# Routing and first-expert gather of a hybrid trunk step: sample tiles taken ahead of the prompt tile, rows gathered from the residual stream

## The chip, the cores and the metric

The kernel runs on one core of one Trainium2 chip. The metric is the device time of one execution in microseconds (us). TensorE, VectorE, ScalarE, GpSimd and SyncE are called PE, DVE, ACT, POOL and SP, as in the profile.

## The reference

One layer of a trunk over 640 tokens of width 1024: 128 prompt tokens and 512 sample tokens, five tiles of 128. The part that matters here begins at the output projection of the token mixers:

```python
x = x + g1 * mix
h2 = _rms_norm(x, p['norm2_g']) * (1 + sc2) + sh2
x = x + g2 * _expert_choice_ffn(h2, p)

logits = (h @ p['w_router']).astype(jnp.float32) + p['b_router'].astype(jnp.float32)
aff = jax.nn.softmax(logits, axis=-1)
gate, idx = lax.top_k(aff.transpose(0, 2, 1), cap)
xs = jax.vmap(lambda hb, ib: hb[ib])(h, idx)
gg = jnp.einsum('becd,edf->becf', xs, p['w_e_gate'])
uu = jnp.einsum('becd,edf->becf', xs, p['w_e_up'])
y = jnp.einsum('becf,efd->becd', jax.nn.silu(gg) * uu, p['w_e_down']) * gate[..., None].astype(h.dtype)
```

Scale and shift (sc2, sh2, g1, g2) differ between prompt and sample. Each of 16 experts takes the 64 sample tokens and the 16 prompt tokens with the highest affinity for it, 80 rows in all, and its weights are 12 MB of float32.

## The kernel before, in words

The order of the work is written out by hand, one instruction stream for each engine, with semaphores between them. A float32 product is made of three products of a high and a low part (`mm3`, lines 1812 to 1814): a high part is a copy on ACT, a low part a subtraction on DVE or POOL.

**Projection.** `w_out` comes in four units of 256 columns. `token_major("out", u, t)` makes one unit for one tile in 24 products; DVE's `residual` (1510 to 1520) multiplies by the gate into `otmp` and adds that to the residual stream `X2`. The last ten jobs follow `OUT_LAST` (97). Between them PE turns each tile's `X2` in two halves (`turn_x2`, 2191), ACT (`first_half`) and DVE (`turned`, 1522) copy these to `x2T`, and `route` (2207) multiplies them by the scaled router matrix into bank 7. The order of tiles is `TILE_ORDER`, the prompt tile last.

**Normalisation.** ACT's `sum_squares` gives each tile's sum, POOL's `rstd2` (648) the reciprocal root. `h2t` is made by DVE for the first three tiles (`modulated`, 1529), and for the other two by POOL and ACT: `scaled` (655), `normalise` (1070), `shifted` (661). ACT stores `X2` (`store_x`, 1077) and `h2t` (`store_h`, 1081) to memory; the later experts gather from there.

**Routing.** One `softmax` (1536) on DVE serves the five tiles and ACT's `softmax_exp` stands in its middle. PE turns the affinities of the first expert into rows (2285), DVE counts for each token how many are ahead of it (`ranks`, 1631) and makes one-hot matrices `hot` and `hot_w`. PE multiplies them with `h2t`: the prompt rows in one step (2295), the sample rows in partial sums (2305) that ACT copies to `parts` (1118) and PE turns and adds (2312). ACT copies the result to `x0f` (`x_raw`, 1120) and its high part to `xTh` (`x_hi`, 1125); DVE makes the low part `xTl` from the bank and `xTh` (`x_lo`, 1625). For the other experts DVE searches the highest values eight at a time (`search`, 1661; 1663 to 1666), and `x_lo(0)` stands after the fifth search.

**First expert.** Units 0, 1 and 5 of the twelve weight units are multiplied in full float32 (`raw_unit`, 2322, line 2329). Units 2, 3 and 4 follow in split form (`gate_up`, 2353). Each waits on `e_lo` for its low part, and these three low parts are POOL's:

```python
            gp.wait_ge(s_idx, 3)
            first_lo(2)
            gp.wait_ge(s_gx, 2)
            for b in range(4):
                gp.wait_ge(s_hst[b], 32 if b == 0 else 16)
            first_lo(3)
            first_lo(4)
```

The buffers of units 3 and 4 lie where `h2t` was, so `first_lo(3)` waits until all five stores of `h2t` have landed (`s_hst`, the fifth tile counted on `s_hst[0]`). SP loads the weight units in order (528 to 551): unit 4 after the last projection, unit 9 after the stores and `s_gx`. `turn_lists` stands in unit 4, after its second chunk.

Of the kernel before, what the change touches and what calls it, by code (L numbers as in the profile page):

```python
# [21 lines left out]
P = 128  # L22
# [21 lines left out]
WARM_0, WARM_A, WARM_B = 14, 1, 6  # L44
# [52 lines left out]
OUT_LAST = [(2, 0), (2, 1), (3, 0), (2, 2), (3, 1), (2, 3), (3, 2), (2, 4), (3, 3), (3, 4)]  # L97
# [73 lines left out]
def trunk(nc, a, outs, consts, scratch):  # L171
# [25 lines left out]
    with ExitStack() as ctx:  # L197
# [126 lines left out]
        TOLD = (7808, 7168, 8752, 9392, 10032)  # L324
# [168 lines left out]
        def _(sp):  # L493
# [34 lines left out]
            def expert(e):  # L528
                first = isinstance(e, int) and e == 0
                for k in (2, 3, 0, 1, *range(4, 12)) if first else range(12):  # L530
# [6 lines left out]
                    elif not first:  # L537
                        sp.wait_ge(e_lo, 12 * e + (k - 11 - len(RAW)))
                    elif k < 2:
                        lo_ready(sp, U_OF[("out", 2 + k)])  # L540
                    elif k == 2:
                        unit_used(sp, U_OF[("conv", 1)])
                    elif k == 4:
                        unit_used(sp, N_U - 1)
                    elif k == 9:
                        sp.wait_ge(s_hst[3], 16)
                        sp.wait_ge(s_xst, 16 * TT)
                        sp.wait_ge(s_t2, 2 * TT)
                        sp.wait_ge(s_nm, 2)
                        sp.wait_ge(s_gx, 2)  # L550
# [19 lines left out]
        def _(gp):  # L570
# [174 lines left out]
        def _(act):  # L745
# [314 lines left out]
            def softmax_exp():  # L1060

                act.wait_ge(s_mx2, 1)
                act.activation(aff[:, 0:TT, 0:E_N], lgs, ACT.Exp).then_inc(s_ex2, 1)
# [17 lines left out]
            def store_h(i):  # L1081
# [3 lines left out]
                else:  # L1085
                    act.wait_ge(s_h2p, 5 - i)
                act.dma_start(h2_d[t * P:(t + 1) * P, :], h2t[i]).then_inc(s_hst[i % 4], 16)

            def first_half(i):
# [3 lines left out]
                act.copy(x2T[:, i % 2], bank[4 + i % 2][:, :].rearrange("p (c t) -> p c t", c=4)).then_inc(s_t2a, 1)  # L1093

# [6 lines left out]
            for i in range(1, 4):  # L1101
                act.wait_ge(s_ssq, TT + i)
                sum_squares(i)
                store_x(i)
                store_h(i - 1)
            act.wait_ge(s_ssq, TT + 4)
            sum_squares(4)
            normalise(3)
            softmax_exp()
            normalise(4)  # L1110
            store_x(4)
            e_hi_unit(0, 2)
            store_h(4)
            e_hi_unit(0, 3)
            store_h(3)
            for hf in range(2):
                act.wait_ge(s_gx, hf + 1)
                act.copy(parts[:, 512 * hf:512 * hf + 512], bank[4 + hf][:, :]).then_inc(s_gs, 1)

            def x_raw():  # L1120
                for hf in range(2):
                    act.wait_ge(e_xt, hf + 1)
                    act.copy(x0f[:, 4 * hf:4 * hf + 4, :], bank[6 + hf][:, 0:4 * M_E].rearrange("p (c t) -> p c t", c=4)).then_inc(e_xr, 1)
# [58 lines left out]
            x_raw()  # L1182
            e_hi_unit(0, 4)
            act.wait_ge(s_hst[0], 32)
            x_hi(0)
# [21 lines left out]
        def _(dve):  # L1207
# [302 lines left out]
            def residual(i, t):  # L1510
# [3 lines left out]
                cols = slice(256 * i, 256 * i + 256)  # L1514
                dve.wait_ge(s_job, n + 1)
                dve.scalar_tensor_tensor(otmp[:, n % 2, :], bank_a(n)[:, 0:256], 0.5, g1bc[:, g, cols], ALU.mult,
                                         ALU.mult).then_inc(s_jd, 1)
                dve.wait_ge(s_jd, freed(n)[1])
                ins = dve.tensor_tensor(X2[:, t, cols], X2[:, t, cols], otmp[:, n % 2, :], ALU.add)
# [16 lines left out]
            def softmax():  # L1536

                y = aff[:, 0:TT, 0:E_N]

                def spread(c):  # L1540
                    return stat[:, c:c + TT].unsqueeze(2).to_broadcast([P, TT, E_N])
# [3 lines left out]
                link(dve.tensor_tensor(lgs, bank[7][:, 0:ROUTE_N * TT].rearrange("p (t e) -> p t e", t=TT)[:, :, 0:E_N], spread(10), ALU.mult))  # L1545
                link(dve.tensor_tensor(lgs, lgs, lb5, ALU.add))
                link(dve.tensor_reduce(stat[:, 36:36 + TT], lgs, AX, ALU.max, negate=True))
                dve.tensor_tensor(lgs, lgs, spread(36), ALU.add).then_inc(s_mx2, 1)
                dve.wait_ge(s_ex2, 1)
                link(dve.tensor_reduce(stat[:, 41:41 + TT], y, AX, ALU.add))  # L1550
                link(dve.reciprocal(stat[:, 46:46 + TT], stat[:, 41:41 + TT]))
                dve.tensor_tensor(y, y, spread(46), ALU.mult).then_inc(s_aff, 1)
# [56 lines left out]
            turned(1)  # L1609
            residual(2, TILE_ORDER[4])  # L1610
            modulated(2)
            residual(3, TILE_ORDER[3])
            turned(2)
            residual(3, TILE_ORDER[4])
            turned(3)
            turned(4)
            softmax()


# [11 lines left out]
            def ranks(t, row, n):  # L1631
# [3 lines left out]
                told = fa[:, TOLD[t]:TOLD[t] + width + P]  # L1635
# [3 lines left out]
                ins = dve.scalar_tensor_tensor(told[:, width:], row[:, n:n + P], v, low, ALU.is_equal, ALU.mult,  # L1639
# [9 lines left out]
            ranks(0, bank[1][:, 0:P], 0)  # L1649
            link(dve.tensor_reduce(rank[:, 0:1], above[:, 0, :], AX, ALU.add))  # L1650
            dve.tensor_tensor(hot_w, slot_p, rank[:, 0:1].to_broadcast([P, CAP_S]), ALU.is_equal).then_inc(s_idx, 1)
            for b in range(2):
                for i in (b, b + 2):
                    ranks(1 + i, bank[0], P * i)
                link(dve.tensor_reduce(rank[:, 1 + b:TT:2], above[:, 1 + b:TT:2, :], AX, ALU.add))
                dve.tensor_tensor(hot[:, b:TT - 1:2, :], slot_p.unsqueeze(1).to_broadcast([P, 2, CAP_S]),
                                  rank[:, 1 + b:TT:2].unsqueeze(2).to_broadcast([P, 2, CAP_S]), ALU.is_equal).then_inc(s_idx, 1)
            dve.wait_ge(s_affp, 2)
            link(dve.tensor_copy(affT, bank[2][0:96, 0:256]))
# [8 lines left out]
            for r in range(CAP_S // 8 - 1):  # L1668
                if r == 5:
# [3 lines left out]
                    x_lo(0)  # L1673
                search(r)

# [133 lines left out]
        def _(pe):  # L1809
# [202 lines left out]
            def token_major(kind, i, t, u):  # L2012
# [5 lines left out]
                for dc in range(DC):  # L2018
                    if kind == "out" and i == 0 and t == TILE_ORDER[0]:
                        pe.wait_ge(s_h, DC + dc + 1)  # L2020
                    last = mm3(bank_a(n)[:, 0:256], hTh[:, dc, x], hTl[:, dc, x], wh[:, dc, :], wl[:, dc, :], dc == 0,
                               dc == DC - 1)
                last.then_inc(s_job, 1)
# [167 lines left out]
            def turn_x2(k, i):  # L2191
# [10 lines left out]
                for c in range(4):  # L2202
                    dc = 4 * k + c
                    last = pe.transpose(bank[4 + q % 2][:, c * P:(c + 1) * P], X2[:, t, dc * P:(dc + 1) * P], ident[:, :])
                last.then_inc(s_t2, 1)

            def route(k, i):
# [6 lines left out]
                for c in range(4):  # L2214
                    x = E_N * ((DC if t == 0 else 0) + 4 * k + c)
                    n = ROUTE_N if x + ROUTE_N <= 2 * DC * E_N else E_N
                    last = pe.matmul(bank[7][:, ROUTE_N * t:ROUTE_N * t + n], x2T[:, q % 2, c, :], wr2f[:, x:x + n],
                                     start=k == 0 and c == 0 and i == 0, stop=k == 1 and c == 3 and i == 4)
# [24 lines left out]
            def last_out(n):  # L2243
# [3 lines left out]
                token_major("out", u, TILE_ORDER[i], out_2 + u - 2)  # L2247
# [12 lines left out]
            last_out(5)  # L2260
            route(0, 4)
            turn_x2(1, 0)
            last_out(6)
            route(1, 0)
            turn_x2(1, 1)
            last_out(7)
            route(1, 1)
            last_out(8)
            turn_x2(1, 2)
            last_out(9)  # L2270
            route(1, 2)
            turn_x2(1, 3)
            turn_x2(1, 4)
            route(1, 3)
            route(1, 4)

            def warm(n, b=1):
# [3 lines left out]
            warm(WARM_0)  # L2281
            pe.wait_ge(s_aff, 1)
            for t in (1, 2, 3, 4, 0):
                out = bank[1][:, 0:P] if t == 0 else bank[0][:, P * (t - 1):P * t]
                last = pe.transpose(out, aff[:, t, 0:1].to_broadcast([P, P]), ident[:, :])
            last.then_inc(s_affp, 1)
            for rows, col, t in ((0, 0, 1), (0, 1, 2), (32, 0, 3), (32, 1, 4), (64, 0, 0), (64, 1, TT)):
                last = pe.matmul(bank[2][rows:rows + 32, col * P:(col + 1) * P], aff[:, t, :], ident[:, :], start=True, stop=True)
            last.then_inc(s_affp, 1)
            warm(WARM_B, 5)  # L2290
            pe.wait_ge(s_idx, 1)
            pe.wait_ge(s_h2p, 1)
            for c in range(DC):
                x0 = (c % 4) * M_E + CAP_S
                pe.matmul(bank[6 + c // 4][:, x0:x0 + CAP_S], h2t[4][:, c * P:(c + 1) * P], hot_w, start=True, stop=True)
                if c % 2 == 1:
                    warm(WARM_A)
            for i in range(2):
                pe.wait_ge(s_idx, 2 + i)
                if i == 1:  # L2300
                    pe.wait_ge(s_h2p, 2)
                for hf in range(2):
                    for g in range(4):
                        tile = i if g < 2 else 2 + i
                        last = pe.matmul(bank[4 + hf][32 * g:32 * g + 32, :], hot[:, tile, 32 * (g % 2):32 * (g % 2) + 32],
                                         h2t[tile][:, 512 * hf:512 * hf + 512], start=i == 0, stop=i == 1)
                    if i == 1:
                        last.then_inc(s_gx, 1)
            for hf in range(2):
                pe.wait_ge(s_gs, hf + 1)  # L2310
                for c in range(4):
                    last = pe.matmul(bank[6 + hf][:, c * M_E:c * M_E + CAP_S], parts[:, (4 * hf + c) * P:(4 * hf + c + 1) * P], twice,
                                     start=True, stop=True)
                last.then_inc(e_xt, 1)

            def first_lists():
                pe.matmul(bank[3][CAP_S:M_E, 0:2], hot_p, aff[:, 0, 0:2 * E_N:E_N], start=True, stop=True)
# [154 lines left out]
```

## Time and profile before

| | us |
|---|---|
| median of 3 runs | 1210.63 |
| lowest and highest | 1210.62, 1211.57 |
| profiled execution, its own time | 1212.05 |
| its span, first to last instruction | 1209.6 |
| PE busy | 1179.1 (97%) |
| DVE busy | 898.7 (74%) |
| ACT busy | 613.1 (51%) |
| POOL busy | 283.5 (23%) |

Times in the trace count from the first instruction. The stretch of the change lies from about 609 to 663: the last projections, the routing, and the first units of the first expert. A row of the timeline gives the start, the time taken, engine, line, operation, output and inputs, shapes and count; brackets hold the idle time of the engine before it and what ended it. The ends of matmuls are modelled and overlap the next start.

### The profile page before, as it was taken

How to read it: one execution, taken by the hardware profiler on the slowest of the kernel's cores; microseconds unless marked ns; L12 is line 12 of the kernel's file. 1: busy time of each engine (PE TensorE's matmuls, PEld its weight loads, DVE VectorE, ACT ScalarE, POOL GpSimd, SP SyncE). 2: the span in 40 equal slices, each digit the busy share in tenths (PEclk: the TensorE clock that was granted, in tenths of full speed). 3: DMA queues.
4: the chain of work that ended last, by engine and by line, in shares of the span. 5: the costliest groups of instructions: out<-in, count | busy, mean ns of one | idle time of the engine just before them, and what ended most of it. 6: DMA issues, size and time to landing. Idle time of an engine off the chain costs nothing.

```text
span 1209.6 us, 18766 instructions
## 1 busy us (share of the span) xinstructions
PE 1179.1 (97%) x7330; PEld 941.3 (78%) x7330; DVE 898.7 (74%) x1047; ACT 613.1 (51%) x710; POOL 283.5 (23%) x189
## 2 busy tenths in 40 slices
PE   5999999999999999999999999999999999999995
PEld 3788899988899999999995666666666666666663
DVE  2689674558877174237568999999999999999997
ACT  3421332245541351322124777777777777777774
POOL 1131030002201143333126212222222112222213
PEclk9999999999999999999999999999999999999998
DMA  9887726221213123444349999999999999999995
GB/s 339 295 240 234 248 64 157 85 99 35 73 36 105 36 71 100 161 158 153 111 174 369 388 379 378 378 380 381 381 386 389 381 377 378 380 381 380 381 387 202
DMA packets 154762, 303.25 MB, mean 251 GB/s; under 512 B 7363, under 2 KB 55527, under 8 KB 154706
## 3 DMA queue, kind: packets, MB, share of 16 engines
q1 hardware_dynamic: 141942, 271.76, 62.1%
q0 software_dynamic: 3968, 12.64, 4.7%
q10 hardware_dynamic: 8796, 18.05, 4.3%
q8 instruction: 41, 0.67, 0.2%
q14 instruction: 15, 0.12, 0.0%
HBM read 285.25 MB, written 17.18 MB: 250 GB/s over the span
## 4 chain that ended last, share of the span: by engine, by line
PE 90%; DVE 5%; issue 1%; DMA 1%; POOL 1%; ACT 0%; SPq 0%; POOLq 0%; ACTq 0%; DVEq 0%
PE bank L1812 17%; PE bank L1813 17%; PE bank L1814 17%; PE bank L1838 5%; PE bank L1841 5%; PE bank L1843 5%; PE bank L1840 5%; PE bank L1842 5%; PE bank L1839 5%; DVE fa L1236 3%; PE bank L2116 1%; DMA wring<-in_w_ada 1%; DVE fa L1328 1%; PE bank L2099 1%; PE bank L2329 1%
## 5 line engine op out<-in xcount | busy, mean ns | idle before, releaser
L1812 PE MATMUL bank<-h2r_a,xTh 128*80 128x512 f32 x368 | 145.4, 395 | 0.0
L1813 PE MATMUL bank<-l2r_b,xTh 128*80 128x512 f32 x368 | 144.7, 393 | 0.0
L1814 PE MATMUL bank<-h2r_a,xTl 128*80 128x512 f32 x368 | 143.4, 390 | 0.0
L693 POOL TENSOR_TENSOR half<-half 1x1 f32<-1x1 f32 x26 | 60.2, 2316 | 287.6 <-DVE ye L1772 286.6
L1236 DVE SCALAR_TENSOR_TENSOR fa<-fa,cwT 128x655 f32<-128x655 f32 x120 | 111.1, 967 | 0.9
L1058 ACT CAST h2r_a<-w_a 128x2048 fp32r<-128x2048 f32 x46 | 88.1, 1914 | 42.9 <-PE bank L1814 42.9
L589 POOL TENSOR_TENSOR lring<-wring,hring 128x2048 fp32r<-128x2048 f32 x15 | 70.2, 4681 | 162.5 <-ACT hring L752 162.5
L1623 DVE TENSOR_TENSOR l2r_b<-w_a,h2r_a 128x2048 fp32r<-128x2048 f32 x45 | 102.8, 2284 | 5.8 <-ACT h2r_a L1058 5.5
L1838 PE MATMUL bank<-hTh,hring 128*128 128x320 f32 x320 | 104.4, 326 | 1.7 <-DVE hTl L1296 0.8
L1843 PE MATMUL bank<-hTh,lring 128*128 128x320 f32 x320 | 98.8, 309 | 0.0
L1841 PE MATMUL bank<-hTl,hring 128*128 128x320 f32 x320 | 98.8, 309 | 0.0
L1840 PE MATMUL bank<-hTl,hring 128*128 128x320 f32 x320 | 98.8, 309 | 0.0
L1842 PE MATMUL bank<-hTh,lring 128*128 128x320 f32 x320 | 98.8, 309 | 0.0
L1839 PE MATMUL bank<-hTh,hring 128*128 128x320 f32 x320 | 98.7, 309 | 0.0
L752 ACT CAST hring<-wring 128x2048 fp32r<-128x2048 f32 (+1 forms) x29 | 54.9, 1893 | 72.9 <-PE bank L1843 45.3
L1814 PEld LDWEIGHTS bank<-h2r_a,xTl 128*80 128x80 f32 x368 | 54.5, 148 | 30.8
L1623 DVE TENSOR_TENSOR l2r_b<-w_b,h2r_a 128x2048 fp32r<-128x2048 f32 x32 | 73.2, 2287 | 6.9 <-ACT h2r_a L1058 6.9
L1812 PEld LDWEIGHTS bank<-h2r_a,xTh 128*80 128x80 f32 x368 | 54.4, 148 | 30.7 <-issue 0.3
L1813 PEld LDWEIGHTS bank<-l2r_b,xTh 128*80 128x80 f32 x368 | 54.4, 148 | 29.3 <-issue 0.3
L1623 DVE TENSOR_TENSOR l2r_a<-w_a,h2r_b 128x2048 fp32r<-128x2048 f32 x30 | 69.1, 2302 | 8.5 <-ACT h2r_b L1058 8.5
L1623 DVE TENSOR_TENSOR l2r_b<-w_r,h2r_a 128x2048 fp32r<-128x2048 f32 x30 | 68.8, 2293 | 5.3 <-ACT h2r_a L1058 3.7
L1058 ACT CAST h2r_a<-w_b 128x2048 fp32r<-128x2048 f32 x32 | 61.2, 1916 | 17.9 <-PE bank L1814 17.9
(433 smaller groups left out, 3205.4 us busy)
## 6 DMA issues: line engine op xcount, KB each, us to landing
w_b<-in_w_e_down SPq DMA_DIRECT2D x48, 1024.0 KB, 14.8
w_e<-in_w_e_up SPq DMA_DIRECT2D x32, 1024.0 KB, 16.8
w_r<-in_w_e_gate SPq DMA_DIRECT2D x32, 1024.0 KB, 16.9
w_a<-in_w_e_gate SPq DMA_DIRECT2D x32, 1024.0 KB, 14.6
w_a<-in_w_e_up SPq DMA_DIRECT2D x32, 1024.0 KB, 14.3
wring<-in_w_in SPq DMA_DIRECT2D x20, 1024.0 KB, 5.1
w_a<-in_w_e_down SPq DMA_DIRECT2D x16, 1024.0 KB, 14.1
fa<-in_w_ada SPq DMA_DIRECT2D x14, 1024.0 KB, 9.0
```

Source lines behind the costliest of these rows:

```text
L1058: act.copy(split_of(e, k)[0], w2[k]).then_inc(e_hi, 1)
L1236: ins = dve.scalar_tensor_tensor(Y[:, c, :], U[:, c, k:k + Y_N], cwT[:, c, k:k + 1], Y[:, c, :], ALU.mult, ALU.add)
L1623: dve.tensor_tensor(low_, w2[k], high.bitcast(F32), ALU.subtract).then_inc(e_lo, 1)
L1812: pe.matmul(out, lh, rh, start=start, stop=False)
L1813: pe.matmul(out, lh, rl, start=False, stop=False)
L1814: return pe.matmul(out, ll, rh, start=False, stop=stop)
L1838: pe.matmul(b0, a_h, xh[:, c, t0], start=st, stop=False)
L1839: pe.matmul(b1, a_h, xh[:, c, t1], start=st, stop=False)
L1840: pe.matmul(b0, a_h, xl[:, c, t0], start=False, stop=False)
L1841: pe.matmul(b1, a_h, xl[:, c, t1], start=False, stop=False)
L1842: pe.matmul(b0, a_l, xh[:, c, t0], start=False, stop=en)
L1843: last = pe.matmul(b1, a_l, xh[:, c, t1], start=False, stop=en)
```

## The change

On PE the jobs (3,3) and (2,4) of `OUT_LAST` are exchanged. The second halves of `route` and `turn_x2`, and the turning of the sample affinities, are put inside the last four projections (`between`). The prompt tile's second half is turned and routed after the first part of the sample rows, into banks 0 and 6. The softmax is split into one for the sample tiles and one for the prompt tile. ACT takes over three of the five second-half copies. The one-hot matrices for the first expert's gather hold each token's reciprocal root, and PE multiplies them with `X2` in place of `h2t`. Scale and shift are applied after the turn: by ACT for the first four chunks, by DVE for the other four, while they copy to `x0f`. The low part is then taken from `x0f` and not from the bank. `normalise(4)` and `store_h(3)` come after the copies of `parts`, `store_h(4)` and the high parts of units 3 and 4 after `x_hi_first`. SP's unit 9 waits for `e_xt` and not for `s_gx`. POOL's `first_lo` part stays as quoted above; ahead of it `shifted(3)` moves before `rstd2(4)`.

```diff
-WARM_0, WARM_A, WARM_B = 14, 1, 6
+WARM_A, WARM_B = 3, 3
-OUT_LAST = [(2, 0), (2, 1), (3, 0), (2, 2), (3, 1), (2, 3), (3, 2), (2, 4), (3, 3), (3, 4)]
+OUT_LAST = [(2, 0), (2, 1), (3, 0), (2, 2), (3, 1), (2, 3), (3, 2), (3, 3), (2, 4), (3, 4)]
...
-                        sp.wait_ge(s_gx, 2)
+                        sp.wait_ge(e_xt, 2)
...
-            for i in range(3):
+            for i in range(4):
                 rstd2(i)
+            gp.wait_ge(s_aff, 1)
             scaled(3)
-            rstd2(3)
+            shifted(3)
             rstd2(4)
             scaled(4)
-            gp.wait_ge(s_aff, 1)
-            for i in (4, 3):
-                shifted(i)
+            shifted(4)
...
+            sample_exp()
+            store_h(2)
+            normalise(3)
             act.wait_ge(s_ssq, TT + 4)
             sum_squares(4)
-            normalise(3)
-            softmax_exp()
-            normalise(4)
+            second_half(4)
             store_x(4)
             e_hi_unit(0, 2)
-            store_h(4)
-            e_hi_unit(0, 3)
-            store_h(3)
+            prompt_exp()
             for hf in range(2):
                 act.wait_ge(s_gx, hf + 1)
                 act.copy(parts[:, 512 * hf:512 * hf + 512], bank[4 + hf][:, :]).then_inc(s_gs, 1)
+            normalise(4)
+            store_h(3)
...
             x_raw()
+            act.wait_ge(s_hst[0], 16)
+            act.wait_ge(s_hst[1], 16)
+            x_hi_first()
+            store_h(4)
+            e_hi_unit(0, 3)
             e_hi_unit(0, 4)
-            act.wait_ge(s_hst[0], 32)
-            x_hi(0)
...
+            residual(3, TILE_ORDER[3])
+            modulated(2)
+            sample_softmax()
             residual(2, TILE_ORDER[4])
...
+                for i in (b, b + 2):
+                    ins = dve.scalar_tensor_tensor(rows_r[:, i, :], slot_p, rank[:, 1 + i:2 + i], stat[:, 11 + i:12 + i].to_broadcast([P, CAP_S]),
+                                                   ALU.is_equal, ALU.mult)
+                ins.then_inc(s_idx, 1)
+                if b == 0:
+                    residual(3, TILE_ORDER[4])
+            prompt_softmax()
...
+            def x_raw():
+                dve.wait_ge(e_xt, 2)
+                for c in range(4):
+                    for g, cols in ((1, slice(0, CAP_S)), (0, slice(CAP_S, M_E))):
+                        ins = dve.tensor_scalar(x0f[:, 4 + c, cols], bank[7][:, c * M_E + cols.start:c * M_E + cols.stop],
+                                                a2c[:, g, 4 + c:5 + c], col40[:, 20 + 8 * g + c:21 + 8 * g + c], ALU.mult, ALU.add)
+                ins.then_inc(s_idx, 1)
+            def x_lo_first():
+                for hf in range(2):
+                    dve.wait_ge(e_xh, hf + 1)
+                    dve.tensor_tensor(xTl[:, 4 * hf:4 * hf + 4, :], x0f[:, 4 * hf:4 * hf + 4, :],
+                                      xTh[:, 4 * hf:4 * hf + 4, :].bitcast(F32), ALU.subtract).then_inc(e_xl, 1)
...
-                    x_lo(0)
+                    x_lo_first()
                 search(r)
+                if r == 0:
+                    x_raw()
...
+            last_out(5)
+            turn_x2(1, 0)
+            route(0, 4)
+            last_out(6, (3, lambda: route(1, 0)))
+            turn_x2(1, 1)
+            last_out(7, (4, third_tile))
+            last_out(8, (3, fourth_tile))
+            last_out(9, (1, sample_turns))
+            sample_rows(0)
+            turn_x2(1, 4)
+            warm(WARM_A, 1)
+            route(1, 4)
+            sample_rows(1)
+            warm(WARM_B, 1)
```

## Rows read from the trace of the kernel before

**Rows 1.** The profile's chain that ended last, shares of the span by engine.
```profile
PE 90%; DVE 5%; issue 1%; DMA 1%; POOL 1%; ACT 0%; SPq 0%; POOLq 0%; ACTq 0%; DVEq 0%
```
**Rows 2.** Timeline of PE, 613 to 660: last projections, routing, first expert.
```profile
613.20 0.61 PE L2204 MATMUL bank<-ident,fa 128*128 128x128 f32 x4
613.56 0.36 PE L1812 MATMUL bank<-hring,hTh 128*128 128x256 f32 x1
...
616.51 1.00 PE L2217 MATMUL bank<-fa 128*128 128x64 f32 x8
617.35 0.61 PE L2204 MATMUL bank<-ident,fa 128*128 128x128 f32 x4
...
631.79 2.64 PE L2279 MATMUL bank<-gtab_h 128*80 128x384 f32 x14
...
644.11 2.00 PE L2312 MATMUL bank<-fa 128*128 128x64 f32 x16
645.95 3.61 PE L2329 MATMUL bank<-w_r,fa 128*80 128x512 f32 x8
...
653.28 0.79 PE L1812 MATMUL bank<-h2r_b,xTh 128*80 128x512 f32 x1
...
659.18 0.40 PE L1812 MATMUL bank<-h2r_a,xTh 128*80 128x512 f32 x1
```
**Rows 3.** Timeline of POOL, 630 to 658.
```profile
630.94 2.38 POOL L659 TENSOR_TENSOR fa<-fa,xg_f 128x1024 f32<-128x1024 f32 x1
...
648.58 4.52 POOL L680 TENSOR_TENSOR l2r_b<-w_e,h2r_a 128x2048 fp32r<-128x2048 f32 x1 [1.74 <-ACT h2r_a L1058]
653.05 4.62 POOL L680 TENSOR_TENSOR l2r_b<-w_a,h2r_a 128x2048 fp32r<-128x2048 f32 x1
```
**Rows 4.** Store issues, window 627 to 650: KB each, us from issue to landing.
```profile
scratch_acc<-fa ACTq DMA_DIRECT2D x1, 512.0 KB, 7.1
...
scratch_h<-xg_f ACTq DMA_DIRECT2D x1, 512.0 KB, 8.1
```
**Rows 5.** Timeline of ACT and its queue, 640 to 644.
```profile
640.21 0.33 ACTq L1087 DMA_DIRECT2D scratch_h<-xg_f  x1
643.39 0.59 ACT L1118 COPY fa<-bank 128x512 f32<-128x512 f32 x1 [3.23 <-PE bank L2305]
```
**Rows 6.** Timeline of DVE, 628 to 652.
```profile
628.41 0.43 DVE L1519 TENSOR_TENSOR fa<-fa,xg_f 128x256 f32<-128x256 f32 x1
...
631.98 0.24 DVE L1545 TENSOR_TENSOR fa<-bank,stat 128x80 f32<-128x80 f32 x1 [1.45 <-PE bank L2217]
632.26 1.17 DVE L1546 TENSOR_TENSOR fa<-fa 128x80 f32<-128x80 f32 x1
...
634.81 0.24 DVE L1552 TENSOR_TENSOR fa<-fa,stat 128x80 f32<-128x80 f32 x1
...
639.44 0.34 DVE L1637 TENSOR_SCALAR_CACHE_REDUCE fa<-bank,fa 128x128 f32<-128x128 f32 x1
...
642.12 0.41 DVE L1659 COPY fa<-bank 96x256 f32<-96x256 f32 x1
642.57 0.42 DVE L1663 MAX8 fa<-fa 96x8 f32<-96x256 f32 x1
...
650.50 0.88 DVE L1628 TENSOR_TENSOR xTl<-bank,xTh 128x320 fp32r<-128x320 f32 x2
```
**Rows 7.** Pieces of the chain, 590 to 700: start, us, what.
```profile
639.40 0.39 PE bank L2295 x4
...
640.57 3.61 PE bank L2305 x32
```
**Rows 8.** Stretch 628 to 648: each engine's busy time, PE clock, DMA share, GB/s.
```profile
628.00:648.00 20.00, 18.62 (x141) 12.66 (x141) 16.17 (x62) 10.64 (x12) 13.09 (x9) 1.00 0.99 367
```
**Rows 9.** Stores of line 1079 from 600 to 630, four of 512 KB.
```profile
DMA to landing us min/median/max: 2.6/2.7/3.6
```
**Rows 10.** Waits of ACT from 620 on: us in total, times, longest us.
```profile
ACT h2r_a L1058 <- PE bank L1814: 91.7, 120, 5.0
```

More of the change, by code:

```diff
@@ L1118, in _, with x_hi_first @@
                 act.copy(parts[:, 512 * hf:512 * hf + 512], bank[4 + hf][:, :]).then_inc(s_gs, 1)
+            normalise(4)
+            store_h(3)
             def x_raw():
-                for hf in range(2):
-                    act.wait_ge(e_xt, hf + 1)
-                    act.copy(x0f[:, 4 * hf:4 * hf + 4, :], bank[6 + hf][:, 0:4 * M_E].rearrange("p (c t) -> p c t", c=4)).then_inc(e_xr, 1)
+                act.wait_ge(e_xt, 1)
+                for c in range(4):
+                    for g, cols in ((1, slice(0, CAP_S)), (0, slice(CAP_S, M_E))):
+                        ins = act.activation(x0f[:, c, cols], bank[6][:, c * M_E + cols.start:c * M_E + cols.stop], ACT.Identity,
+                                             bias=col40[:, 16 + 8 * g + c:17 + 8 * g + c], scale=a2c[:, g, c:c + 1])
+                    ins.then_inc(e_xr, 1)
+            def x_hi_first():
+                act.wait_ge(e_xr, 4)
+                act.copy(xTh[:, 0:4, :], x0f[:, 0:4, :]).then_inc(e_xh, 1)
+                act.wait_ge(s_idx, 5)
+                act.copy(xTh[:, 4:8, :], x0f[:, 4:8, :]).then_inc(e_xh, 1)
             def x_hi(n):
@@ L1543, in softmax, with prompt_softmax @@
+            def prompt_softmax():
                 dve.wait_ge(s_lg, 2 * TT)
                 dve.wait_ge(s_r2, TT)
[L1545 to L1548, printed above, removed]
@@ new lines, in _ @@
+            dve.tensor_tensor(hot, slot_p.unsqueeze(1).to_broadcast([P, TT - 1, CAP_S]),
+                              rank[:, 1:TT].unsqueeze(2).to_broadcast([P, TT - 1, CAP_S]), ALU.is_equal)
+            dve.wait_ge(s_affp, 2)
+            ranks(0, bank[0][:, 0:P], 0)
+            link(dve.tensor_reduce(rank[:, 0:1], above[:, 0, :], AX, ALU.add))
+            dve.scalar_tensor_tensor(rows_rp, slot_p[:, 0:CAP_P], rank[:, 0:1], stat[:, 10:11].to_broadcast([P, CAP_P]), ALU.is_equal,
+                                     ALU.mult).then_inc(s_idx, 1)
@@ L2022, in token_major @@
                                dc == DC - 1)
+                    if between is not None and dc == between[0]:
+                        between[1]()
                 last.then_inc(s_job, 1)
@@ L2246, in last_out @@
                     out_unit(3)
-                token_major("out", u, TILE_ORDER[i], out_2 + u - 2)
+                token_major("out", u, TILE_ORDER[i], out_2 + u - 2, between)
             last_out(0)
@@ L2259, in _, with warm, third_tile, fourth_tile @@
                 route(0, n - 1)
[L2260 to L2277, printed above, removed]
+            def warm(n, b):
                 for _ in range(n):
                     pe.matmul(bank[b][0:M_E, 0:384], gtab_h[:, 0:M_E], gtab_h[:, :], start=True, stop=True)
[L2281 to L2301, printed above, removed]
+            def third_tile():
+                route(1, 1)
+                turn_x2(1, 2)
+            def fourth_tile():
+                turn_x2(1, 3)
+                route(1, 2)
+                route(1, 3)
+            def sample_turns():
+                pe.wait_ge(s_aff, 1)
+                for t in range(1, TT):
+                    last = pe.transpose(bank[2][:, P * (t - 1):P * t], aff[:, t, 0:1].to_broadcast([P, P]), ident[:, :])
+                last.then_inc(s_affp, 1)
+            def sample_rows(i):
+                pe.wait_ge(s_idx, 1 + i)
                 for hf in range(2):
@@ L2311, in _ @@
                 for c in range(4):
-                    last = pe.matmul(bank[6 + hf][:, c * M_E:c * M_E + CAP_S], parts[:, (4 * hf + c) * P:(4 * hf + c + 1) * P], twice,
+                    pe.matmul(bank[6 + hf][:, c * M_E:c * M_E + CAP_S], parts[:, (4 * hf + c) * P:(4 * hf + c + 1) * P], twice,
                                      start=True, stop=True)
-                last.then_inc(e_xt, 1)
+            warm(WARM_B, 2)
+            pe.wait_ge(s_idx, 3)
+            for c in range(DC):
+                x0 = (c % 4) * M_E + CAP_S
+                last = pe.matmul(bank[6 + c // 4][:, x0:x0 + CAP_P], X2[:, 0, c * P:(c + 1) * P], rows_rp, start=True, stop=True)
+                if c % 4 == 3:
+                    last.then_inc(e_xt, 1)
             def first_lists():
+                pe.wait_ge(s_idx, 4)
                 pe.matmul(bank[3][CAP_S:M_E, 0:2], hot_p, aff[:, 0, 0:2 * E_N:E_N], start=True, stop=True)
```

106 lines of the change are left out of this document (66 added, 40 removed).

## The prediction

> **What bounds the kernel now.** I read the chain of waits first: nine tenths of it is PE [rows 1], so a change is worth what it does to the time at which PE's gapless work for the experts begins. Then the timeline of PE from the last projections to that point, to see where it begins: unit 2 of the first expert starts at 653.28 and the first product of unit 4 at 659.18 [rows 2]. From there on the view of waits has no wait of PE until the last expert, so every microsecond by which unit 4's start moves should move the end. ACT's casts of weights wait for PE, 91.7 us in all [rows 10], and for no load: the weights come early enough.
>
> Third, POOL, because units 2 to 4 need low parts that it makes. Its subtraction for unit 3 runs from 648.58 and the one for unit 4 from 653.05 for 4.62 [rows 3]. Unit 4's low part is thus ready at 657.67 and PE takes it at 659.18: 1.5 us of slack, no more. What starts this pair is a store: the last `store_h` is issued at 640.21 [rows 5] and lands 8.1 later [rows 4], at 648.3, and POOL starts 0.25 after that. So two chains end at the first expert: PE's rows, and store, POOL, unit 4.
>
> Last, what DVE and POOL hold in turn; I call it the port. The tensor_tensor of line 1546, with both inputs in SBUF, takes 1.17 where its neighbours of the same size take 0.24 [rows 6]; it started in the middle of a POOL instruction that ran from 630.94 to 633.32 [rows 3] and ended just behind it. `x_lo` at 650.50 [rows 6] runs inside POOL's subtraction and takes 0.88 for two: it reads the bank, not two SBUF operands.
>
> **The change, part by part.**
> *PE's projections.* Until 613.56 nothing but a swap of a route and a turn. A projection takes 2.95 (613.56 to 616.51), a route 0.84, a turn 0.36 [rows 2]. The sample logits are complete after two and a half projections, four routes, three turns and some 0.4 of waits and draining: 613.56 + 7.4 + 3.4 + 1.1 + 0.4 = 625.8. The last projection ends near 630.7, after the remaining one and a half (4.4) and 0.5 for turning the affinities and waiting for them.
>
> *Sample routing on DVE.* The softmax took 631.98 to 635.05, 3.07, of which 0.93 was the port (1.17 less 0.24) [rows 6]. POOL waits for it now and leaves the port free: 2.14, so 628.0. The residual of (2,4), two instructions of 0.43 [rows 6], to 628.9. A pair of ranks with its one-hot matrix took 639.44 to 642.12, 2.68 [rows 6]: first pair at 631.6, residual of (3,4) at 632.5, second pair at 635.3. The second residual term reads the bank, so POOL's `shifted(3)` does not stop it.
>
> *PE behind it.* Half the sample rows from 631.7 (16 products took 3.61 [rows 7], so 1.8), turn 0.4, ACT's copy 0.6 [rows 5] with 0.3 of hand-off, which covers the first three warming products, and route 0.84: 635.7. The other half, 637.5. Three warming products at 0.19 (2.64 for 14 [rows 2]), 638.05. DVE and ACT have made the prompt softmax by 637.7, so it costs nothing: the second half of the rows hides it. Turning the prompt affinities 0.75, warming 0.6, adding the parts 1.84 (644.11 to 645.95 [rows 2]), warming 0.6: 641.8. The prompt rows, 16 pieces at 0.39 for four [rows 7], 1.5: 643.3. The prompt's ranks on DVE are done before, near 639.6.
>
> *What PE gains.* Two raw units and the first lists took 645.95 to 653.28, 7.3 [rows 2]; from 643.3 that is 650.6. This is the gain the head offers: 2.7.
>
> *What DVE gives back.* DVE's `x_raw` stands in the search, after round 0, and waits for the prompt rows: 643.5 plus eight small instructions of about 0.14 (the trace has none of this form; between 0.1 and 0.25 each), 644.65. All later searches stand behind it. Five searches with what follows took 642.57 to 650.50 [rows 6], 7.93, so four take 6.3: `x_lo_first` starts at 651.0 and ends at 651.9. Unit 2 needs it: at most 1.4 of the 2.7 is left.
>
> *The store.* `store_h(4)` now stands on ACT behind `x_hi_first`, whose second cast waits for DVE's `x_raw`: issued at 644.8 and no longer at 637.9. A store of 512 KB landed in 2.6 with idle queues [rows 9], and in 7.1 and 8.1 with the weights in flight [rows 4]; the DMA share is 0.99 in that stretch [rows 8]. Units 4 to 8 are issued 3 us later now, so the queues are as full at 645. I take 7.1, the store that had its ring to itself, as this one has; the ends are 2.6 and 8.1. It lands at 651.9. POOL starts 0.25 later, takes 4.55 twice [rows 3], and unit 4's low part is there at 661.25; PE starts on it at 661.4. Before: 659.18. **That is 2.2 us later**, and unit 3 has waited too.
>
> *Without a price.* SP's unit 9 waits for `e_xt`, 643.3, and for `store_h(3)`, issued at 638.4 and landing by 645.5; before it left at 648.3, so the loads behind it are not later. Units 4 to 8 come 3 us later, under the cover of the casts' waits for PE [rows 10]. The full `hot` and the lists lie in DVE's waits for PE. `turn_lists` in unit 4 needs the end of the search, near 661.6, and is reached at 662.8. Nothing of unit 5 or later waits for more than before.
>
> **The sum.** 2.2 on the profiled execution's 1212.05 is 1214.25; that execution lies 1.4 above the median of the runs, and on 1210.63 the same 2.2 gives **1212.8**.
>
> One rule is weighed here. In this stretch the trace shows 7.1 and 8.1 from issue to landing for 512 KB [rows 4]. The Trainium skill (DMA: Bandwidth & Descriptors, section "Anatomy of one DMA — SWDGE (gpsimd) path") gives a constant 2.0 us plus bytes over 436 GB/s, fitted on the other kind of queue, which is 3.2 here; that agrees with the idle rows, not with these. By it the sum would be 0.2 and not 2.2; the rival below stands on rows alone.
>
> **The rivals.** What a measurement can tell from no change is 0.2%, 2.4 us.
>
> *The port is lost* (22%). `x_lo_first` reads `x0f` and `xTh`, two SBUF operands. If the store lands before 651.0, POOL's subtraction has the port when DVE arrives, and a DVE instruction of this form ends behind POOL's [rows 3, 6]. If POOL's next subtraction follows without a gap, as it does in the trace (653.05 after 648.58 plus 4.52), DVE waits out both: store at 650.5, port free at 659.9, unit 2 starts at 660.9, 7.1 after the 653.8 at which it had PE to itself before. Time 1217.7. If DVE gets in between, the loss is 2 to 3, as in the forecast. For it: the two arrive within a microsecond of each other. Against: a landing of 7.1 comes just after.
>
> *No change* (12%): the store lands in about 3.3, at 648.1, nearer the idle 2.6. POOL then runs 648.35 to 652.9, DVE slips in until 653.8 and POOL's second ends at 658.4. Unit 2 starts at 653.9, which is when the raw unit's last product was out before (653.28 and 0.5 of overlap), and unit 4 finds its low part: 0.2 or less, 1210.8. It decides at a landing of 648.5 or earlier. Against: share 0.99.
>
> *The head's gain is kept* (8%): the hand-offs of the head are shorter than in my walk by 2 us and the store lands early, so that unit 4 starts by 656.8: 1208.2. It decides at a low part of unit 4 ready by 656.7. It can't be much less, as `x_lo_first` alone allows 1.4 by this walk.
>
> **How the numbers follow.** The forecast (58%) spans 1211.8 to 1214, for 0.4 to 1 us either way in the landing and in my hand-offs; somewhat under half of it lies over 1213.05. Slower by over 0.2%: 26% of it and the 22%, 48%. Within: 32% and 12%, 44%. Faster: 8%. The range reaches from 1209.8 (part of the third rival, the second) to 1217.9 (the first).
>
> **What would show it.** In the trace of the changed kernel: raw units from 643 to 651; `store_h(4)` near 645, landing near 652; POOL's line of `first_lo` for unit 3 starting 0.25 behind it; PE idle ahead of units 3 and 4, released by POOL; unit 4 near 661. Wrong would be: PE without a wait there, a landing under 4 us, `x_lo_first` long past 1 us (first rival), or a PE wait later on a weight load, which would mean that the loads had become the bound.

## The result, and the profile after

The changed kernel takes 1214.67 us (median of 7 runs, 1213.91 to 1215.91); the kernel before, beside it, takes 1210.63 (7 runs, 1210.38 to 1212.22). The ratio is 1.0028, with a 95% interval of 1.0019 to 1.0037: slower by some 3.4 us; the two medians differ by 4.0. The profiled execution of the changed kernel took 1214.50 with a span of 1212.7. Span against span the loss is 3.1.

The timeline of TensorE in the changed kernel, from the prompt rows to unit 4 (it answers to [rows 2]):

```profile
642.25 1.85 PE L2381 MATMUL bank<-fa 128*128 128x16 f32 x16
644.05 5.33 PE L2402 MATMUL bank<-w_r,fa 128*80 128x512 f32 x8
...
650.00 3.66 PE L2402 MATMUL bank<-w_r,fa 128*80 128x512 f32 x8
653.12 0.77 PE L1873 MATMUL bank<-h2r_b,xTh 128*80 128x512 f32 x1
...
657.76 0.46 PE L1873 MATMUL bank<-h2r_a,xTh 128*80 128x512 f32 x1 [1.34 <-POOL l2r_b L682]
...
662.30 0.46 PE L1873 MATMUL bank<-h2r_a,xTh 128*80 128x512 f32 x1 [1.54 <-POOL l2r_b L682]
```

Unit 4 starts at 662.30 where it started at 659.18: 3.1 later, as much as the span is longer. Ahead of units 3 and 4 TensorE now waits for GpSimd. GpSimd's timeline in the same execution (it answers to [rows 3]):

```profile
642.19 4.51 POOL L682 TENSOR_TENSOR l2r_a<-w_e,h2r_b 128x2048 fp32r<-128x2048 f32 x1
653.12 4.58 POOL L682 TENSOR_TENSOR l2r_b<-w_e,h2r_a 128x2048 fp32r<-128x2048 f32 x1 [6.42 <-DMA scratch_h<-fa]
657.66 4.58 POOL L682 TENSOR_TENSOR l2r_b<-w_a,h2r_a 128x2048 fp32r<-128x2048 f32 x1
```

It stood 6.42 ahead of unit 3's subtraction, until the store of the prompt's h had landed. ScalarE and its queue show when that store left:

```profile
643.25 2.31 ACT L1142 ACTIVATE fa<-bank,fa 128x64 f32<-128x64 f32 x8 [3.45 <-PE bank L2381]
645.67 0.46 ACT L1148 CAST xTh<-fa 128x320 fp32r<-128x320 f32 x1
646.16 0.46 ACT L1150 CAST xTh<-fa 128x320 fp32r<-128x320 f32 x1
646.17 0.33 ACTq L1094 DMA_DIRECT2D scratch_h<-fa  x1
```

It was issued at 646.17, with the second cast, and landed 6.83 later, at 653.00. The program holds the store behind two things: ScalarE's own scalings of the first four chunks, which ended at 645.56 (the first row), and VectorE's `x_raw` for the other four, which ended at 646.13. VectorE's `x_raw` and `x_lo_first` are these rows:

```profile
644.22 1.91 DVE L1710 TENSOR_SCALAR fa<-bank,fa 128x64 f32<-128x64 f32 x8 [2.28 <-PE bank L2381]
...
652.19 0.88 DVE L1717 TENSOR_TENSOR xTl<-fa,xTh 128x320 fp32r<-128x320 f32 x2
```

The first eight raw products take 5.33 where they took 3.61 [rows 2]. The view by stretches of the changed kernel says why (the third column from the end is the granted clock):

```profile
643.00:644.00 1.00, 1.00 (x10) 1.00 (x10) 0.00 (x0) 0.75 (x3) 1.00 (x1) 1.00 1.02 406
644.00:646.00 2.00, 2.00 (x4) 0.76 (x5) 1.78 (x8) 1.89 (x7) 2.00 (x1) 0.54 1.05 396
646.00:648.00 2.00, 2.00 (x4) 0.56 (x3) 1.86 (x8) 1.97 (x3) 0.70 (x1) 0.60 1.06 420
```

Behind the narrow products of the prompt rows the clock falls to its lower level (1.2 in place of 2.4 GHz) for most of that raw unit.

A second thing has moved by as much as unit 4: the stream of weights, that is, SyncE's loads of the weight units in their order. The last unit of the last expert before, by source line (issue, then time to landing):

```profile
L551 SPq DMA_DIRECT2D w_b<-in_w_e_down x1: 1027/1027/1027, 1162.5 to 1162.5; - x1
...
DMA to landing us min/median/max: 17.8/17.8/17.8
```

and after:

```profile
L554 SPq DMA_DIRECT2D w_b<-in_w_e_down x1: 1027/1027/1027, 1165.6 to 1165.6; - x1
...
DMA to landing us min/median/max: 17.7/17.7/17.7
```

It lands at 1180.3 before and at 1183.3 after. ScalarE's cast of it, before and then after:

```profile
1182.59 1.91 ACT L1058 CAST h2r_b<-w_b 128x2048 fp32r<-128x2048 f32 x1
```

```profile
1185.72 1.91 ACT L1060 CAST h2r_b<-w_b 128x2048 fp32r<-128x2048 f32 x1
```

So in both kernels the weights are 2.3 to 2.4 ahead of their use. Two explanations thus fit the same 3.1: the chain of store, GpSimd and unit 4, and the stream. With the clock and VectorE's low part that makes four to tell apart.

All work ahead of the difference shifts from one execution to the next. GpSimd's `shifted(4)`, for example, starts at 639.88 in the changed kernel and between 639.06 and 640.89 in the experiments made from it. Where that matters I subtract the difference and call it the shift.

### The profile page after: what moved, and what is told of

Same layout as the page of the kernel before. It is cut to its first block, busy times and chain, and to the rows that moved or that the text cites. A ratio compares the mean times of both kernels' runs of the same rounds, so it can differ in the third digit from the quotient of the medians.

```text
span 1212.7 us, 18766 instructions
## 1 busy us (share of the span) xinstructions
PE 1179.7 (97%) x7318; PEld 940.6 (78%) x7318; DVE 901.6 (74%) x1060; ACT 616.5 (51%) x721; POOL 284.7 (23%) x189
## 4 chain that ended last, share of the span: by engine, by line
PE 88%; DVE 6%; DMA 2%; issue 2%; POOL 1%; ACT 1%; SPq 0%; POOLq 0%; ACTq 0%; DVEq 0%
PE bank L1873 17%; PE bank L1874 17%; PE bank L1875 16%; PE bank L1899 5%; PE bank L1901 5%; PE bank L1900 5%; PE bank L1904 5%; PE bank L1903 5%; PE bank L1902 5%; DVE fa L1266 3%; PE bank L2179 1%; DMA wring<-in_w_ada 1%; DVE fa L1358 1%; PE bank L2162 1%; PE bank L2152 1%
```

## The experiments

**e2_store_late: the store behind two casts.**

```diff
-            store_h(4)
             e_hi_unit(0, 3)
             e_hi_unit(0, 4)
+            store_h(4)
```

> The store of the prompt's h goes behind the two casts of weights on ScalarE's queue: issued at about 648.4 for 646.17. Theory (landing, then two subtractions of 4.58 us, then unit 4): landing at about 655.2 for 653.00, unit 4 at 664.5 for 662.30, +2.2 us, about 1216.9. Rival (x_lo_first and the port): no change, as VectorE's order is the same. Second rival (the clock): no change.

Measured: ratio 1.0023 (1.0014 to 1.0032), no change against the changed kernel. The timeline of ScalarE and its queue in this run says that nothing had been tried:

```profile
646.85 0.46 ACT L1150 CAST xTh<-fa 128x320 fp32r<-128x320 f32 x1
646.86 0.33 ACTq L1094 DMA_DIRECT2D scratch_h<-fa  x1
647.22 1.89 ACT L1060 CAST h2r_a<-w_e 128x2048 fp32r<-128x2048 f32 x1
```

The store stands behind both weight casts in the program and is issued before the first one starts, at the same point as in the changed kernel (shift 0.7). The run is a repetition of the changed kernel, and as such it settles what the slow raw unit costs: here the granted clock stays at 1.00 from 643 to 650, the first raw unit takes 3.63, and the time is the same. TensorE's row for that unit:

```profile
644.75 3.63 PE L2402 MATMUL bank<-w_r,fa 128*80 128x512 f32 x8
```

In the changed kernel the 1.7 us of the slow raw unit cost nothing, as TensorE then waits for GpSimd anyway.

**e3_low_early: VectorE's low part ahead of the search.**

```diff
-                    x_lo_first()
                 search(r)
                 if r == 0:
                     x_raw()
+                    x_lo_first()
```

> VectorE makes the low part of the first expert's rows right behind x_raw, at about 646.7 for 652.19, while GpSimd has the port only till 646.7. Theory: no change within 0.5 us, 1214.7, as the store's landing still starts the subtractions. Rival (x_lo_first and the port): faster by 1 us or more, with the subtractions shorter or earlier. Second rival (the clock): no change; the raw products keep their half clock.

Measured: 1.0027 (1.0016 to 1.0038), no change, though the low part is now made at 645.35:

```profile
645.35 1.30 DVE L1717 TENSOR_TENSOR xTl<-fa,xTh 128x320 fp32r<-128x320 f32 x2
```

The late `x_lo_first` is not the bound. TensorE waits 3.04 for unit 3 in this execution, and in that wait the granted clock falls: it is 0.50 from 657 to 661. GpSimd's low part for unit 4 is ready at 661.39, and unit 4 starts at 662.15.

**e1_no_store_wait: no wait for stores ahead of unit 3's low part.**

```diff
-            for b in range(4):
-                gp.wait_ge(s_hst[b], 32 if b == 0 else 16)
             first_lo(3)
+            gp.wait_ge(s_hst[2], 16)
+            gp.wait_ge(s_hst[3], 16)
             first_lo(4)
+            gp.wait_ge(s_hst[0], 32)
+            gp.wait_ge(s_hst[1], 16)
```

> Both low parts still follow the cast of their weights, but only the last waits for any store: the first for none, the second for the stores of tiles 2 and 3, which had landed at 644.9 in the changed kernel. Theory (the landing of the last store of h starts GpSimd's last two subtractions, and the second of these starts unit 4): the subtraction for unit 3 starts at 648.4, with the cast of its weights, and ends at 653.0; the one for unit 4 ends at 657.6 to 658.5; unit 4 starts at 659.5 to 659.8 where it was at 662.30, now behind TensorE's own units 2 and 3, so -2.5 to -2.8 us against the changed kernel, about 1212.0. One thing can take most of that away: x_lo_first comes to VectorE at 652.2, inside the subtraction; if only its first half gets in between the two, its second half comes at 658.2, unit 3 at 658.7 and unit 4 at about 662: -0.4 us. Rival (x_lo_first, late in VectorE's search, is what the units wait for, the store only happened to land then): no gain, within 0.4 us. Second rival (the half clock of the raw products is the loss): no gain, as unit 2 starts with the end of the raw products at 653.1 all the same.

Measured: slower still, 1.0046 (1.0032 to 1.0059). No theory had said so; the trap had been named, and priced too low: only unit 3 was to wait for the second half of VectorE's low part, but the program has unit 2 wait for both halves. GpSimd's timeline in this run:

```profile
649.46 4.52 POOL L682 TENSOR_TENSOR l2r_b<-w_e,h2r_a 128x2048 fp32r<-128x2048 f32 x1 [1.87 <-ACT h2r_a L1062]
653.93 4.76 POOL L682 TENSOR_TENSOR l2r_b<-w_a,h2r_a 128x2048 fp32r<-128x2048 f32 x1
```

The summary of VectorE's `x_lo_first` by source line (duration least, median, most in ns, then first and last start):

```profile
L1719 DVE TENSOR_TENSOR xTl<-fa,xTh x2: 1255/3016/4776, 653.1 to 654.3; 128x320 fp32r<-128x320 f32 x2
...
  PE bank L1875: 6.2, 1
```

The subtractions ran early, as meant. VectorE arrived at 653.08 inside the first one. Its first half got in between the two, the second half came up in the second one, took 4.776 where 0.44 is its own time (0.88 for two in the changed kernel), and ended just behind it. Unit 2 needed it, so TensorE waited 6.2. In that wait the granted clock fell: it was 0.50 from 657 to 663, and from the start of unit 2 to that of unit 3 it took 4.93 where it took 3.16 in the kernel before. The wait for the store had kept the port free for VectorE: taking away a wait that bound gave one that was worse.

**e4_both: the edits of e1 and e3 together.**

> The two edits together: no store is waited for ahead of the subtraction for unit 3, and x_lo_first goes behind x_raw. Theory: subtractions 648.4 to 653.0 and 653.0 to 657.6, with nothing on VectorE that wants the port for them; units 2, 3 and 4 one behind the other on TensorE from the end of the raw products: 653.1, 656.4, 659.7, so -2.6 us, about 1212.1; where the raw products keep the full clock, 1.7 us more, 1210.4. Rival (x_lo_first and the port): the gain is that of moving x_lo_first alone. Second rival (the clock): the gain comes only if the granted clock of 644 to 648 is back at 1.00.

Measured: 1.0035 (1.0022 to 1.0049); nothing gained. The timeline of TensorE shows unit 4, and a new wait at the other end of the kernel:

```profile
658.19 0.46 PE L1875 MATMUL bank<-h2r_a,xTh 128*80 128x512 f32 x1 [0.29 <-POOL l2r_b L682]
...
1193.42 0.46 PE L1875 MATMUL bank<-h2r_a,hTh 128*80 128x512 f32 x1 [3.68 <-DVE hTl L1788]
```

Unit 4 came at 658.19, 4.5 earlier with the shift of 0.4. That gain went in the last expert. ScalarE's timeline there:

```profile
1179.54 1.92 ACT L1062 CAST h2r_a<-w_b 128x2048 fp32r<-128x2048 f32 x1 [1.73 <-DMA w_b<-in_w_e_down]
1182.09 1.92 ACT L1062 CAST h2r_a<-w_b 128x2048 fp32r<-128x2048 f32 x1 [0.63 <-DMA w_b<-in_w_e_down]
...
1191.38 1.06 ACT L1180 ACTIVATE w_a<-fa 128x1024 f32<-128x1024 f32 x1 [1.69 <-DMA fa<-scratch_acc]
...
1192.44 0.41 ACT L1171 CAST hTh<-bank 128x320 fp32r<-128x320 f32 x1
```

The casts now wait for the weights. Then the squares of the final norm wait for the sums, which are loaded behind the weights, and the cast of hT, whose low part TensorE needs, stands behind those squares. The stream was 2.4 us behind the units, and beyond that it takes over.

**e9_store_wait: the store really late.** The wait that e2 lacked:

```diff
-            store_h(4)
             e_hi_unit(0, 3)
             e_hi_unit(0, 4)
+            act.wait_ge(e_hi, lows(0, 4))
+            store_h(4)
```

> The changed kernel, with the prompt's h stored only once ScalarE has ended both weight casts that followed it: a semaphore wait ahead of the store, since its place in the program alone did not move the issue (e2_store_late: 646.86 us). Issue at 650.2 for 646.17, +4.1. Theory (landing, two subtractions, unit 4): landing at about 657.1, unit 4 at about 666.4 for 662.30, and the units after it follow: +4.1 us, about 1218.8. Rival (the stream of weights sets the end: its last landing is at 1183.3 and its last cast at 1185.7): the first 2.4 us or less of any delay are not the stream's, so the end moves by 1.7 us or by nothing. Rival (x_lo_first and the port): nothing.

Measured: 1.0058 (1.0045 to 1.0072), median 1218.96. GpSimd's timeline and then TensorE's:

```profile
656.86 4.49 POOL L682 TENSOR_TENSOR l2r_b<-w_e,h2r_a 128x2048 fp32r<-128x2048 f32 x1 [10.23 <-DMA scratch_h<-fa]
```

```profile
661.41 0.72 PE L1874 MATMUL bank<-h2r_a,xTh 128*80 128x512 f32 x1 [5.39 <-POOL l2r_b L682]
...
665.93 0.46 PE L1874 MATMUL bank<-h2r_a,xTh 128*80 128x512 f32 x1
```

Issued at 650.17, the store landed 6.6 later and unit 4 started 3.63 later than in the changed kernel. The span is 3.6 longer. What unit 4 is late by goes through to the end in full, so the chain of store, GpSimd and unit 4 sets the end of the changed kernel.

**e6_stream: the weights 2 us or more earlier.** The unit that takes the place of the third output unit's low part no longer queues behind the last output job:

```diff
+        EARLY_K = 7 + H_SLOT[U_OF[("out", 2)]]
...
-                for k in (2, 3, 0, 1, *range(4, 12)) if first else range(12):
+                for k in (2, 3, 0, 1, EARLY_K, *(k for k in range(4, 12) if k != EARLY_K)) if first else range(12):
...
+                    elif k == EARLY_K:
+                        unit_used(sp, U_OF[("out", 2)])
                     elif k == 4:
                         unit_used(sp, N_U - 1)
```

> The changed kernel, with one edit on SyncE: the one of the first expert's units whose place is the low part of the third output unit is loaded when that unit has been used (about 628.2), ahead of the four that wait for the last output job (631.25). The queue is empty from 626 to 631, so every later weight lands up to 2.7 us earlier, the last at about 1180.6 for 1183.3. Theory (the landing of the store, two subtractions, unit 4): no change, 1214.7 within 0.5, as unit 4 stays at 662.3. Rival (the change moved the stream 3.3 us back, and the stream sets the end): -2.7 us, about 1212.0. Both bounds, one close behind the other (2.4 us in the changed kernel): no change here either, and a gain only where both are moved.

Measured: 1.0029 (1.0018 to 1.0039), no change, though the last weights are now issued at 1163.7, land 16.1 later and are cast at 1187.25, so 7.4 ahead of their use. GpSimd's row for unit 3, then TensorE's first products of units 3 and 4:

```profile
653.70 4.54 POOL L686 TENSOR_TENSOR l2r_b<-w_e,h2r_a 128x2048 fp32r<-128x2048 f32 x1 [7.68 <-DMA scratch_h<-fa]
```

```profile
658.29 0.72 PE L1877 MATMUL bank<-h2r_a,xTh 128*80 128x512 f32 x1 [2.85 <-POOL l2r_b L686]
...
663.50 0.63 PE L1877 MATMUL bank<-h2r_a,xTh 128*80 128x512 f32 x1
```

In the changed kernel the stream alone is not the bound: with the weights this early the end still follows unit 4. But unit 4 did not stay at 662.30, as had been expected. The store, issued at 645.48, landed 8.1 later, and in the wait of 2.85 the granted clock fell: it was 0.50 from 658 to 664. Whether the edit made the store late is not shown: with the same edit it landed in 8.0 in e7, 7.1 in e8 and 5.9 in e10.

**e7_both_stream: both bounds moved** (the edits of e4 and e6).

> The edits of e4_both and of e6_stream together: unit 4 at about 657.6 (it was so in e4_both), and the stream 2.7 us earlier. In e4_both the end did not move: the last three units waited for their landing, and TensorE 3.7 us for a low part behind ScalarE's squares, which waited for rows loaded behind the weights. If these two bounds are the whole story: the last unit lands at about 1181.9, the wait of 3.7 us shrinks by 2.7 to about 1, and the time is 3 to 4 us under the changed kernel, 1210.7 to 1211.7. If the stream is not what held e4_both, no more than e4_both: 1214.7 to 1216.4.

Measured: 1210.96, ratio 0.9991 (0.9982 to 1.0000): some 4.5 us under the changed kernel by the ratios, and level with the kernel before or just under it. ScalarE's timeline in the last expert, where e4 waited:

```profile
1182.29 1.91 ACT L1066 CAST h2r_b<-w_b 128x2048 fp32r<-128x2048 f32 x1
...
1188.32 0.41 ACT L1175 CAST hTh<-bank 128x320 fp32r<-128x320 f32 x1
```

No wait for weights is left there, and TensorE has none for hT. The two bounds are the story of e4.

**e8_tail: e7 with the cast of hT ahead of the final squares.**

```diff
+                    h_hi(e, 1)
                     for i in range(3):
                         final_square(i)
-                    h_hi(e, 1)
...
-                    final_mean(0, 3)
                     h_lo(e, 1)
+                    final_mean(0, 3)
```

> e7_both_stream, and in the last expert the second hT cast goes ahead of ScalarE's three final squares, and its low part ahead of VectorE's mean. The wait of TensorE for the low part of hT, 3.7 us in e4_both, goes whatever the loads do. By the trace of e4_both VectorE's final scaling ended only 0.57 us ahead of the rows' first product, so no more than 0.6 us is to be had against e7_both_stream: 1210.2 to 1211.7. If the rows of the last tiles were not the next limit, up to 1.7 us more, as TensorE then has no pause of 3.7 us there, after which its granted clock was half for 8 products in e4_both.

Measured: 1.0011 (1.0002 to 1.0020), some 2.4 us worse than e7, where level or up to 0.6 better had been expected. ScalarE's timeline:

```profile
1187.45 0.43 ACT L1175 CAST hTh<-bank 128x320 fp32r<-128x320 f32 x1 [3.52 <-PE bank L2468]
1187.77 1.06 ACT L1184 ACTIVATE w_a<-fa 128x1024 f32<-128x1024 f32 x1
```

In e7 ScalarE spends this stretch on the squares (1184.73 to 1188.3); now all three come behind a wait of 3.52. From the last weight cast to the end of the span it is 29.5 (1182.02 to 1211.5) where e7 has 27.0 (1182.29 to 1209.3). In this execution the first raw unit again ran at the lower clock (5.33), and from its start to the last weight cast 1.2 more went by than in e7 (643.61 to 1182.02 against 645.06 to 1182.29). That fits a clock which costs where no wait hides it, but one execution is all that shows it.

**b_stream: the kernel before, with the edit of e6.**

> The kernel before, with the edit of e6_stream alone: the unit whose place is the low part of the third output unit is loaded as soon as that unit has been used, ahead of the four that wait for the last output job (627.95). Theory (in the kernel before the chain of units sets the end and the stream is 2.3 us behind it: last landing 1180.3, last cast 1182.6): no change, ratio 0.999 to 1.001, though the last landing moves 1 to 2.7 us ahead. Rival (the stream was already the bound of the kernel before, so that its later start alone explains the loss): faster by 2 us or more, ratio 0.998.

Measured: 1.0001 (0.9992 to 1.0011). The last weights land at 1178.5 (issued at 1162.4, 16.1 to landing) in place of 1180.3, and nothing changes. The stream was not the bound before either.

**e10_no_warm: e7 without the last six warming products.**

```diff
-            warm(WARM_B, 2)
...
-            warm(WARM_B, 2)
```

> e7_both_stream without the last two groups of three warming products, which take 0.59 and 0.56 us of TensorE's time on the way to the first raw product (640.41 to 641.00, 642.70 to 643.26). If the granted clock stays at 1.00: the raw products, the casts that follow the same copies, and with them the units start 1.15 us earlier; the last weights, 1.0 us behind in e7_both_stream, leave about 1.0 us of it: ratio to e7_both_stream 0.999, about 1210.0. If the clock falls in the raw products as it did in the changed kernel (5.33 us for the first eight in place of 3.63): +1.7 - 1.15 = +0.5 us, about 1211.5.

Measured: 1209.42, ratio 0.9985 (0.9976 to 0.9994): the one version whose interval lies wholly below the kernel before. It is not told apart from e7 (0.9982 to 1.0000). The clock stays at 1.00 in its execution, from 640 to 668. TensorE's timeline:

```profile
642.46 3.63 PE L2406 MATMUL bank<-w_r,fa 128*80 128x512 f32 x8
...
656.17 0.46 PE L1879 MATMUL bank<-h2r_a,xTh 128*80 128x512 f32 x1 [0.30 <-POOL l2r_b L686]
```

From the start of the raw unit to unit 4 it is 13.7, as in e7 (645.06 to 658.79). ScalarE's timeline in the last expert:

```profile
1178.66 1.91 ACT L1066 CAST h2r_a<-w_b 128x2048 fp32r<-128x2048 f32 x1 [1.20 <-DMA w_b<-in_w_e_down]
```

The stream is the bound again; while it is, what TensorE gains beyond this in the first expert does not reach the end. Whether the kernel before would gain from fewer warming products as well was not tried.

## Why the prediction was right

The direction, the mechanism and most of the size were right. It gave +2.2 us; the spans differ by 3.1 and the ratio gives 3.4. The median, 1214.67, lies 0.7 over the span that the forecast gave itself (1211.8 to 1214), inside the whole range.

- *Where the end is set.* "Every microsecond by which unit 4's start moves should move the end": 3.12 and 3.1 here, 3.63 and 3.6 in e9. From unit 4's first product to the end of the span it is 550.4 to 550.5 in seven versions (the kernel before, b_stream, the changed kernel, e1, e2, e7 and e9), whether unit 4 starts at 658.79 (e7) or at 666.78 (e1). It is 550.7 in e3 and e6, where the clock was still low when unit 4 began, and longer only where the weights came late (e4 554.8, e10 552.6) or the tail was changed (e8 552.9).
- *The head.* The sample softmax was to end at 628.0, the first pair of ranks at 631.6, the second at 635.3; the trace has 628.4, 631.9 and 635.6. The prompt rows were to start at 641.8 and end at 643.3; they start at 642.25 and the raw products at 644.05. From this start the changed kernel is 1.9 ahead of the one before, not 2.7, and of the 1.4 that was left to unit 2 it kept 0.2 (653.12 for 653.28).
- *The mis-sized terms* stand ahead of the store. `x_raw` on VectorE was "eight small instructions of about 0.14", from 643.5 to 644.65. They take 0.24 each, at the top of the bounds given, and start 0.7 later: 644.22 to 646.13. ScalarE's half of the same work had no term: its eight instructions take 2.31 and end at 645.56, and the store stands behind them too. So with VectorE started as it was and as quick as forecast, which is 645.4, the store would still have left some 0.8 late. It leaves at 646.17 where 644.8 was forecast, 1.4 late.
- *The landing.* 7.1 was taken, 6.83 came; in the other versions this store took from 5.9 (e10) to 8.1 (e6). "7.1 and 8.1" [rows 4] were not all of that view: it has a third store, the prompt's h itself, in 6.3 (`scratch_h<-fa ACTq DMA_DIRECT2D x1, 512.0 KB, 6.3`). That one and the 8.1 were both issued with another store still under way, the 7.1 was not, so the reason given for 7.1 does not order these rows. The rival of no change, which needed a landing of some 3.3, falls. By the fit of the Trainium skill (DMA: Bandwidth & Descriptors, "Anatomy of one DMA — SWDGE (gpsimd) path") the estimate for this size is 3.2 us. That is less than half of what was measured; the measurement decides.
- *GpSimd.* 0.12 after the landing where I had 0.25, then 4.54 to the next start and 4.58 where I had twice 4.55; unit 4 at 662.30 where I had 661.4. The 0.9 is the late store's 1.4, less 0.3 of landing and 0.2 of hand-offs.
- *The lost port.* It did not happen, by 0.8 us: `x_lo_first` started at 652.19 and the store landed at 653.00. Both stand behind `x_raw` and came 1.1 to 1.2 later than forecast, so the narrow gap stayed. e1 shows that the rival is real: 0.46%, some 5.6 us by the ratio and 7.6 by the spans, where 7.1 had been given; some 1.8 of it goes by the lower clock (4.93 for 3.16 in unit 2), which the rival had not counted. "DVE waits out both" was wrong in part: one of its two instructions gets in between. The Trainium skill (SBUF — State Buffer, "SBUF: two separate sides") has a VectorE instruction with two SBUF inputs and a GpSimd instruction that reads SBUF exclude each other for whole instructions, the first one to start keeping the port. The 4.776 in e1 agrees.
- *Units 4 to 8 later, without a price.* Right in that the stream alone holds neither kernel (e6, b_stream), but "the weights come early enough" was read from the waits of all experts together [rows 10]. At the last expert the cover is 2.3 us, and the change moved the stream by 3.0. So the change put back two bounds by 3 us at once, and undoing one gave nothing (e4, and e6 with its late store) until the other was undone as well (e7).

What stays open: why the granted clock fell in the raw products of two executions (the changed kernel and e8) and not in the other seven that have the same products in front of them (e1, e2, e3, e4, e6, e7 and e9).

## What to carry to other kernels

A step that is moved takes its DMA with it: look up what waits for that DMA, here the three low parts on another engine, and what that wait in turn had been keeping apart. Where a change puts off a stream of loads under cover, read the cover at its thinnest place, the last use, and not from the sum of all waits; a second bound 2 us behind the first can make each single repair look useless. When a repair shows nothing, look first whether the trace shows the edit at all: e2 had moved a line of the program and no event.

## What was not expected of the hardware

- A store was issued before the casts ahead of it in the program had started: 646.86 against 647.22 in e2. Only a wait on the casts' semaphore put it behind them (650.17 in e9).
- Between two back-to-back subtractions on GpSimd (649.46 and 653.93 in e1) one waiting VectorE instruction got in; the next one had to wait out the second subtraction.
- The clock fell to its lower level behind 16 products of 16 columns although TensorE had hardly paused, in some executions only; in the one execution of e10, without six of the warming products, it stayed up. It fell too in TensorE's waits for unit 2 or 3: 2.85 in e6, 3.04 in e3, 5.39 in e9 and 6.23 in e1.
